# A sixth place for half an up pair in the second later expert layer, where the memory's keys and values lay

## The reference, cut to what matters

```python
for i in range(DEPTH):
    ...
    xa = memory_cross_attention(q, mem, w_kv[i])
    o = jnp.concatenate([tok, xa], axis=-1) @ w_out[i]
    x = layer_norm(ALPHA * x + o, ln1_g[i], ln1_b[i])
    f = grouped_moe(x, router_w, router_b, w_gate[i], w_up[i], w_down[i])
    x = layer_norm(ALPHA * x + f, ln2_g[i], ln2_b[i])
```

## Time and profile before

| | |
|---|---|
| median of three runs | 2265.35 us (2263.66 to 2267.38) |
| the profiled execution's own time | 2267.8 us |
| its span, first to last instruction | 2266.2 us |
| what lies around the span | 1.6 us |
| TensorE busy | 2062.8 us (91%) |
| VectorE, ScalarE, GpSimd busy | 496.4, 367.6, 116.4 us |
| bytes moved by DMA | 644.26 MB, mean 284 GB/s |
| mean granted TensorE clock | 0.959 of full speed |
| last up load landed, as the chain has it | at 2231.73 us |

### The profile page before, as it was taken

The page is one execution under the profiler, slowest core; times in us unless marked ns, Lnnn a source line. Parts: engine busy times, 40 slices in busy tenths (PEclk is TensorE's granted clock), DMA queues, the critical chain, the costliest instruction groups (busy, mean ns, idle before and its releaser), DMA issues.

```text
span 2266.2 us, 30000 instructions
## 1 busy us (share of the span) xinstructions
PE 2062.8 (91%) x12470; PEld 1004.3 (44%) x12470; DVE 496.4 (22%) x1255; ACT 367.6 (16%) x845; POOL 116.4 (5%) x275
## 2 busy tenths in 40 slices
PE   5989999999999989999999999869799958979994
PEld 2574547777677443222222222235433316643331
DVE  2143841000159220000000001012411113231112
ACT  2022432000341221000100000012111102011100
POOL 2000000000000100000000000000000100000010
PEclk9999999999999999999999999979899989979997
DMA  9241359442773579999999999971699984189994
GB/s 327 75 149 44 143 177 359 145 136 97 252 264 122 212 274 366 402 410 398 403 400 410 409 399 412 413 273 38 279 418 422 421 337 163 37 351 423 422 416 171
DMA packets 192025, 644.26 MB, mean 284 GB/s; under 512 B 11635, under 2 KB 44875, under 8 KB 156043
## 3 DMA queue, kind: packets, MB, share of 16 engines
q1 hardware_dynamic: 165440, 469.92, 54.4%
q0 software_dynamic: 25824, 172.09, 18.6%
q10 hardware_dynamic: 619, 0.23, 0.0%
HBM read 641.15 MB, written 1.05 MB: 283 GB/s over the span
## 4 chain that ended last, share of the span: by engine, by line
PE 74%; DMA 12%; SPq 6%; DVE 4%; issue 2%; ACT 2%; DVEq 0%; ACTq 0%; POOLq 0%
PE bank L1366 12%; PE bank L967 12%; PE bank L978 9%; PE bank L1403 8%; PE bank L1349 7%; PE bank L1274 7%; DMA ring<-in_w_up 6%; SPq L759 5%; DMA ring<-in_l_moe_w 5%; PE bank L1285 3%; PE bank L1322 3%; PE bank L1434 2%; PE bank L1591 1%; PE bank L1310 1%; DMA ring<-in_l_mod_w 1%
## 5 line engine op out<-in xcount | busy, mean ns | idle before, releaser
L1366 PE MATMUL bank<-ring,wide 128*32 128x512 f32 x3520 | 412.8, 599 | 23.8 <-DMA ring<-in_l_moe_w 22.2
L1403 PE MATMUL bank<-dreg,RB 128*32 128x512 f32 x2592 | 316.0, 607 | 9.7 <-DMA dreg<-in_l_moe_w 4.8
L1366 PEld LDWEIGHTS bank<-ring,wide 128*32 128x32 f32 x3520 | 108.5, 110 | 278.1 <-issue 248.6
L1349 PE MATMUL bank<-ring,wide 128*32 128x512 f32 x1408 | 175.3, 621 | 39.1 <-DMA ring<-in_w_up 37.8
L978 PE MATMUL bank<-wide,ring 128*128 128x256 f32 x832 | 183.0, 381 | 0.2 <-ACT wide L1853 0.2
L3002 DVE TENSOR_TENSOR H<-SG,bank 128x256 f32<-128x256 f32 x82 | 34.7, 423 | 676.0 <-ACT SG L2084 676.0
L978 PEld LDWEIGHTS bank<-wide,ring 128*128 128x128 f32 x832 | 158.6, 191 | 22.8 <-issue 0.9
L1403 PEld LDWEIGHTS bank<-dreg,RB 128*32 128x32 f32 x2592 | 79.6, 111 | 193.9 <-issue 186.1
L967 PE MATMUL bank<-ring,wide 128*128 128x512 f32 x352 | 159.5, 610 | 1.2 <-DMA ring<-in_w_kv 1.1
L1274 PE MATMUL bank<-wide,ring 128*128 128x256 f32 x704 | 153.7, 379 | 0.8 <-DVE MODX L2515 0.8
L1274 PEld LDWEIGHTS bank<-wide,ring 128*128 128x128 f32 x704 | 133.7, 190 | 23.0 <-issue 4.3
(11 more groups left out here) (444 smaller groups left out, 1608.4 us busy)
## 6 DMA issues: line engine op xcount, KB each, us to landing
ring<-in_l_moe_w SPq DMA_DIRECT2D x120, 1024.0 KB, 16.3
dreg<-in_l_moe_w POOLq DMA_DIRECT2D x88, 1024.0 KB, 8.7
dreg<-in_w_down POOLq DMA_DIRECT2D x64, 1024.0 KB, 12.8
ring<-in_w_gate SPq DMA_DIRECT2D x56, 1024.0 KB, 11.9
ring<-in_w_up SPq DMA_DIRECT2D x56, 1024.0 KB, 17.3
ring<-in_l_mod_w SPq DMA_DIRECT2D x24, 2048.0 KB, 8.3
ring<-in_l_moe_w SPq DMA_DIRECT2D x40, 768.0 KB, 11.6
ring<-in_l_ffn_w SPq DMA_DIRECT2D x22, 1024.0 KB, 10.5
```

The lines of the kernel that those rows point to most:

```text
L1349: mm = pe.matmul(banks[r % 2][32 * g:32 * g + 32, :].rearrange("p (w n) -> p w n", w=2), tokens_of(m.order[i][0], c, k), w, start=k == 0, ...
L1366: mm = pe.matmul(banks[r % 3][32 * g:32 * g + 32, :].rearrange("p (w n) -> p w n", w=2), tokens_of(m.order[i][0], c, k), quads[:, s, :, k ...
L1403: mm = pe.matmul(banks[4 + 2 * m.lane(m.unit(m.order[i][0])) + h][32 * g:32 * g + 32, :], HQ[:, r % 4, j, 32 * q:32 * q + 32], dring[:, i ...
```

## The change

Layer B gets a place 5, columns 0 to 4095 of arena. For its loads below 24 the places go round as 0, 1, 2, 3, 4, 5; from load 24 on as `always[n % 5]` of 0, 1, 2, 3, 5. The first load into a place (load 5 into place 5) waits for nothing of its own. The number of layer B's down loads ahead of the two rows of the last layer norm is worked out for layer B. Layer A keeps its places. The semaphore gate_pad goes, and its wait on VectorE with it; masks_made, which GpSimd gives later, stays.

```diff
-SLOTS2 = RING + 1
+SLOTS2 = RING + 2
...
         self.pairs = self.blocks // 2
+        self.spare_home = name == "B"
...
-        n |= {f"up_in{s}": self.loaded(*self.in_slot(s)[-1]) for s in range(SLOTS2)}
+        n |= {f"up_in{s}": self.loaded(*self.in_slot(s)[-1]) if self.in_slot(s) else 0 for s in range(SLOTS2)}
...
     def slot(self, q, h):
 
         n = self.halves.index((q, h))
-        return n % SLOTS2 if n < 4 * SLOTS2 else n % RING
+        always = [0, 1, 2, 3] + [5] * self.spare_home
+        first = [0, 1, 2, 3] + [4] + [5] * self.spare_home
+        return first[n % len(first)] if n < 4 * len(first) else always[n % len(always)]
...
-        half_slots = [pairs[:, s, :, :, :] for s in range(RING)] + [carve(RSf, 0, 2, KC // 2, NCH)]
+        half_slots = [pairs[:, s, :, :, :] for s in range(RING)] + [carve(RSf, 0, 2, KC // 2, NCH), carve(arena, 0, 2, KC // 2, NCH)]
...
                     elif n == RING:
                         sp.wait_ge(sem("x_updated"), updated)
-                    else:
+                    elif (q, h) != here[0]:
                         last_q, last_h = here[here.index((q, h)) - 1]
...
-            step(pool.memset(WG[:, :, :], 0.0), "gate_pad")
+            step(pool.memset(WG[:, :, :], 0.0))
...
             pool.wait_ge(sem("x_updated"), 7)
+            lead = rows_lead(MOEB)
             down_loads(pool, MOEB, lambda e: A["w_down_2"][1, e], range(lead))
...
-            dve.wait_ge(sem("gate_pad"), 1)
             dve.wait_ge(sem("masks_made"), 1)
```

## The result

The changed kernel has a median of 2275.34 us over four runs (2272.25 to 2277.25), the kernel before 2265.99 over its four. The ratio is 1.0041 with an interval of 1.0024 to 1.0058: slower by 0.41%, or 9.3 us, where +10.4 us and 2275.8 us were forecast. The profiled execution took 2276.81 us, its span is 2275.2 us, 9.0 above that of before.

What follows compares the result with a forecast made beforehand. DMA bounds the stage's end: load 24's stall makes load 31 land 10.4 us later, with nothing taken for load 5 by itself or gate_pad. From the median, 2265.35 + 10.4 = 2275.8 us; range 2270 to 2282.

Steps and rivals of the forecast that it cites:

- What bounds it: End of the stage: DMA at 419 GB/s without reserve sets it, with a fixed tail of 34.5 us behind load 31.
- Load 5 without a wait: Start of layer B's up loads: issued about 2005.2, not 2019.66, filling 5.0 us of a DMA hole; nothing by itself.
- Load 24 behind load 23: SP queue, place 5: load 24 waits for round 10's upper half, so is issued at 2179.88, not 2157.83.
- Round 11's lower half: Its up loads 24 and 25 land at 2201.6, so it starts 7.9 us late.
- Round 11's upper half: Its up loads 26 and 27 land at 2216.1, so it starts 18.0 us late.
- Its clock: Round 11's upper half on TensorE: at the lower clock after idling it takes about 5.7 us, ending at 2221.8.
- Load 31: Last up load of the stage: lands at 2242.1 instead of 2231.73, +10.4 us.
- The norm rows: Two rows of the last norm, behind down load 25: they add 1.05 MB to the DMA ledger, 2.5 us.
- A load's fixed time and rate: DMA loads: the skill's 2.0 us plus bytes over 436 GB/s would end 2.3 us sooner; the stage shows 419 GB/s.
- The whole heap at the end: Rival, stage tail: same stall, but load 31 lands with the whole heap at 2246.0; +14.3 us, 2279.7 us, chance 0.12.
- Two thirds for SP: Rival, DMA sharing after the stall: SP's burst gets two thirds of the rate; +7.4 us, 2272.8 us, chance 0.04.
- The faster outcome: Rival, DMA hole at load 5: filling it reaches the end; 5.0 us faster, at most 8.2, chance 0.05.

Runs made afterwards that it cites:

- the change with the rows last: The changed kernel with the two rows of the last norm issued behind the last down load, not behind down load 25: 2270.77 us, ratio 1.0024.
- the shifted rotation: The changed kernel with the place order shifted from load 24 on, so load 24 waits for round 8's lower half: 2257.57 us, ratio 0.9969.
- the hold to round 9's upper half: The shifted rotation with SP waiting for round 9's upper half ahead of load 24: 2264.67 us, ratio 0.9999 against the kernel before.

## Why the prediction was right, step by step

- **What bounds it.** DMA sets the end of the stage and has no reserve: right. The stretch behind 2182 is without a gap in the change, and the tail stayed (34.5 and 34.9 us).
- **Load 5 without a wait, nothing by itself.** Right: 4.5 us of DMA time were won, and the kernel that keeps only this (place 5 up to load 23) is at -1.1 us, not clear of zero. TensorE's round 10 ended within 1 us of where it did. The interval of that kernel reaches to -3.2 us, so a small worth is not excluded.
- **Load 24 behind load 23.** Right in place and time: issue forecast at 2179.88, found at 2179.69, with the wait proved by the kernel before with nothing but this hold (+6.6) and by its removal (-7.0).
- **Round 11's lower half.** Forecast 2201.6, found 2198.44, 3.2 us too late. Two sizes were off, both of how the queues share, and both to the same side. POOL's queue came in later than the 1.4 us that I gave it: its load is issued at 2181.29, and up to 2185.2 every byte is SP's, 3.9 us. The kernel before had it too, 3.4 us from 2182.10 on, and the 1.4 stood on no row. And the half share holds for packets, not for bytes:

```profile
q1 hardware_dynamic: 110, 0.84, 100.8%
...
q1 hardware_dynamic: 116, 0.88, 70.6%
q0 software_dynamic: 47, 0.39, 30.8%
...
q1 hardware_dynamic: 267, 1.95, 59.4%
q0 software_dynamic: 269, 1.31, 41.0%
```

  Queues of the changed kernel from 2182 to 2184, 2184 to 2187 and 2198 to 2206 (packets, MB, share). In the last the packets are even, 267 and 269, the megabytes are not, 1.95 and 1.31: the norm rows are moved by smaller packets. Where only down and up loads meet, the bytes are even again, here in the change with the rows last, from 2190 to 2204:

```profile
q0 software_dynamic: 411, 2.98, 51.0%
q1 hardware_dynamic: 404, 2.92, 49.8%
```

  The Trainium skill ("DMA: Bandwidth & Descriptors", Queues, rings and completion order) says that each engine goes round the queues that have work packet by packet. These rows agree.
- **Round 11's upper half.** Forecast 2216.1, found 2216.15. What the up queue won early, the down queue wanted later: the heap's total sets this time, not the split.
- **Its clock.** Forecast 5.7 us for the half, found 6.35 after 12.74 us of idle, with a granted clock of 0.50 from 2210 to 2220; the lower half needed 5.0 us after 5.48. The last down loads went out from 2227.15 on (forecast 2226.5).
- **Load 31.** Forecast 2242.1, found 2240.26; +10.4 and found +8.5 in the trace, 9.3 in the medians. The same slow start of POOL's queue: issued at 2227.15, it moves nothing until 2230.8, where I had 2228, and each us gives the up queue 0.21 MB more. By the ledger that alone lands load 31 2.8 us sooner than forecast; it was 1.8.
- **The norm rows.** 2.5 us forecast; 2.1 in the traces of the change with and without them. The medians give 3.9 there and 2.5 for the shifted rotation, both with intervals that overlap. **gate_pad**: nothing seen; load 4 is issued at 2003.83, where it was at 2004.39. It was not tried alone.
- **A load's fixed time and rate.** The Trainium skill ("DMA: Bandwidth & Descriptors", Anatomy of one DMA), which the prediction cites, states its 2.0 us and 436 GB/s for loads that GpSimd issues. The loads that this stage waits for are SP's, and both queues together move 420 GB/s here. The sum did not use the page's figures. The prediction puts 2 us behind the last byte, from 2229.7 on; in the trace the up queue still moved 0.07 MB from 2230 to 2231 and one packet after it, so a part of these 2 us is the end of the bytes, and the agreement with the page shows less than it seems to.
- **The rivals.** The whole heap at the end (+14.3) did not come, for the reason given, the late restart. Two thirds for SP (+7.4) lies nearer to the trace's +8.5 than my 10.4: in the tail the up queue did get the larger part, by POOL's late start. Its mechanism, late down loads, did not come: the change's downs wait for none. The faster outcome needed load 24 not to be behind load 23, and the shifted rotation is exactly that; it gave -7.0, where I had -5.0, at most -8.2. The terms missing there are the last 1.7 us of the kernel before, in which DMA had nothing left to move, and a little of load 28, which a place from outside round 11 lets go early.

The forecast lay 1.9 us above the trace and 1.1 us above the medians; that it is nearer to the medians is chance, for they carry a scatter of 5 us.

Not settled: why the hold to round 9's upper half costs 6.8 us in the medians for 4.5 us more of idle DMA, when its one trace shows 4.0. The two kernels ran on different chips, each compared with the kernel before on its own, and the near ends of the two intervals lie 2.2 us apart, so 4.0 fits them too. Whether the late down load is there in all runs was not tried.

## What to carry to other kernels

When a ring of places changes its length in the middle of a stream, list for each load the holder that it waits for; a load that follows its own predecessor into a place stops the whole in-order queue, and the free places behind it count for nothing. A prefetch hold shows as missing DMA rate while TensorE is fully busy; here DMA stood still some 30 us before anything waited. In a DMA-bound tail, ask first which of the queued bytes are wanted last, and issue them last: that gave about as much here (9.7 us) as two megabytes more of room (7.0 us), and the two gains add up only in part.

## What the runs showed of the hardware that was not expected

- Two queues with work share by packets: 267 and 269 packets were 1.95 and 1.31 MB while a broadcast of rows was among them, and 404 and 411 packets were 2.92 and 2.98 MB without it.
- A load on GpSimd's queue starts late when SP's queue is full. In the change, a down load issued at 2181.29 moved nothing until 2185.2, and one issued at 2227.15 nothing until 2230.8. With nothing else on the way it is quick: one issued at 2168.10 had its first packets at 2169.2, and SP's load 24, issued at 2179.69, at 2180.6. Whether the full queue is the cause was not tried.

```profile
2168.10 0.53 POOL L638 DMA_DIRECT2D dreg<-in_w_down  x1 [14.95 <-PE bank L1407]
...
q0 software_dynamic: 6, 0.05, 225.0%
```

  The issue, and the down queue from 2169.2 to 2169.4.
- Runs of one kernel scatter by 3 to 9 us here (2256.78 to 2260.18 for one, 2253.04 to 2262.22 for another), as much as most of the effects in question; only sets of runs tell them apart. Part of it comes ahead of the stage: in the twelve traces load 4 is issued between 1998.40 and 2004.39.
